# Keys, values and penalties of a dilated prompt attention stored by residue class mod 16

## What is computed

```python
DILATED_PATTERNS = ((128, 1), (512, 4), (2048, 16))
for win, dil in DILATED_PATTERNS:
    nw = win // dil                      # 128 keys per window, for each pattern
    # tokens split in dil residue classes; within a class, blocks of nw queries
    # see the block of keys before and their own, banded to dist 0..nw
    s = jnp.einsum('brnqhd,brnkhd->brnhqk', qb, kc).astype(f32) * scale + bias
    ...
    outs.append(o); lses.append(lse)
return combine_patterns(outs, lses)      # weighted by the softmax denominators
```

## Time and profile before

| What | us |
|---|---|
| median of 3 runs | 3155.96 |
| the profiled execution | 3153.91 |
| its span | 3152.2 |
| TensorE busy, mean granted clock | 2876.6, 0.947 |
| VectorE, ScalarE, GpSimd busy | 1235.5, 887.1, 192.6 |

### The profile page before, as it was taken

The page is one execution under the profiler, slowest core; times in us unless marked ns, Lnnn a source line. Parts: engine busy times, 40 slices in busy tenths (PEclk is TensorE's granted clock), DMA queues, the critical chain, the costliest instruction groups (busy, mean ns, idle before and its releaser), DMA issues. The chain is left out here.

```text
span 3152.2 us, 49398 instructions
## 1 busy us (share of the span) xinstructions
PE 2876.6 (91%) x17770; PEld 1632.3 (52%) x17770; DVE 1235.5 (39%) x2977; ACT 887.1 (28%) x2188; POOL 192.6 (6%) x476
## 2 busy tenths in 40 slices
PE   7998887673989898996997999999999999999998
PEld 6655665452657474765443444444444444444444
DVE  6326555564646465564443222222112221122134
ACT  6116666222434343443222110111001210011111
POOL 2000000100112020211110000000000000000000
PEclk9999889886989898997998999999999999999999
DMA  5121222752010201102322102111231112311035
GB/s 179 75 93 39 81 61 58 225 172 65 15 49 8 56 16 42 34 10 78 138 93 80 40 20 110 41 40 40 88 131 41 40 40 93 127 41 40 33 126 177
DMA packets 177965, 231.40 MB, mean 73 GB/s; under 512 B 12561, under 2 KB 141924, under 8 KB 177148
## 3 DMA queue, kind: packets, MB, share of 16 engines
q1 hardware_dynamic: 173142, 216.53, 21.4%
q0 software_dynamic: 4656, 12.65, 1.3%
HBM read 160.08 MB, written 69.07 MB: 73 GB/s over the span
## 5 line engine op out<-in xcount | busy, mean ns | idle before, releaser
L2312 DVE TENSOR_TENSOR f_hidden<-f_silu,f_ps_up 128x512 f32<-128x512 f32 (+1 forms) x110 | 65.2, 593 | 627.5 <-ACT f_silu L2253 627.5
L113 PE MATMUL f_ps_gate<-act_hi,f_w_hi 128*128 128x512 bf16 (+1 forms) x880 | 285.5, 343 | 11.1 <-DVE f_w_lo L2299 9.5
L113 PE MATMUL f_ps_y<-f_down_hi,f_h_hi 128*128 128x512 bf16 (+1 forms) x748 | 284.3, 380 | 8.5 <-issue 6.4
L114 PE MATMUL f_ps_gate<-act_lo,f_w_hi 128*128 128x512 bf16 (+1 forms) x880 | 285.4, 343 | 0.0
L115 PE MATMUL f_ps_gate<-act_hi,f_w_lo 128*128 128x512 bf16 (+1 forms) x880 | 285.2, 343 | 0.0
L114 PE MATMUL f_ps_up<-act_lo,f_w_hi 128*128 128x512 bf16 (+1 forms) x880 | 284.6, 342 | 0.0
L115 PE MATMUL f_ps_up<-act_hi,f_w_lo 128*128 128x512 bf16 (+1 forms) x880 | 284.6, 342 | 0.0
L113 PE MATMUL f_ps_up<-act_hi,f_w_hi 128*128 128x512 bf16 (+1 forms) x880 | 284.6, 342 | 0.0
L114 PE MATMUL f_ps_y<-f_down_lo,f_h_hi 128*128 128x512 bf16 (+1 forms) x748 | 284.3, 380 | 0.0
L115 PE MATMUL f_ps_y<-f_down_hi,f_h_lo 128*128 128x512 bf16 (+1 forms) x748 | 284.1, 380 | 0.0
L2253 ACT ACTIVATE f_silu<-f_ps_gate 128x512 f32<-128x512 f32 (+1 forms) x110 | 57.1, 519 | 656.6 <-PE f_ps_up L115 656.6
(11 more groups left out here) (360 smaller groups left out, 5483.0 us busy)
## 6 DMA issues: line engine op xcount, KB each, us to landing
y_part_rows<-f_total SPq DMA_DIRECT2D x48, 512.0 KB, 2.6
f_total<-y_part_rows SPq DMA_DIRECT2D x48, 512.0 KB, 3.5
f_raw_gate<-in_w_gate SPq DMA_DIRECT2D x22, 512.0 KB, 4.5
f_raw_up<-in_w_up SPq DMA_DIRECT2D x22, 512.0 KB, 5.9
f_raw_down<-in_w_down SPq DMA_DIRECT2D x22, 512.0 KB, 3.6
m_w_raw<-in_w_in SPq DMA_DIRECT2D x20, 512.0 KB, 5.1
s_comb<-pattern_rows SPq DMA_DIRECT2D x24, 396.0 KB, 4.4
nx<-in_x_prompt SPq DMA_DIRECT2D x16, 512.0 KB, 3.5
```

What stands on the lines that cost most here:

```text
L113: pe.matmul(out, w_hi, x_hi, start=first, stop=False)
L114: pe.matmul(out, w_hi, x_lo, start=False, stop=False)
L2312: nc.vector.tensor_tensor(hidden[u][:, 0:n], act_out[u][:, 0:n], ps_up[u][:, 0:n], ALU.mult).then_inc(hidden_done, 1)
```

## The change

Keys of the prompt are stored by residue class mod 16: class r takes 128 neighbouring places, in order of token. A key block of pattern 0 is then 16 runs of 8 keys, one of pattern 1 four runs of 32, one of pattern 2 one run of 128. Values are loaded so that their rows match that order, and the table of penalties has its columns permuted. Pattern 1 still reads its queries with stride 4; for pattern 2 GpSimd copies the queries of a pair to class order (`a_q_cls`). Penalties are loaded per sequence instead of per pair, and two waits on the new semaphore `q_sorted` are added.

```diff
+RUN = (P // CLASSES, P * DILATIONS[1] // CLASSES, P)
+def key_run(keys, pat, r, b, n):
     dil = DILATIONS[pat]
+    return keys.rearrange("p (a r b i) -> p r b a i", r=dil, b=TILES // dil, i=RUN[pat])[:, r, b:b + n, :, :]
...
-                    if dil == 1:
-                        sp.dma_start(v[k % 2][:, :, :], rows.rearrange("(b i) c -> i b c", i=P)).then_inc(v_in[k % 2], 16)
-                        return
-                    for b in range(TILES // dil):
-                        src = rows[b * P * dil:(b + 1) * P * dil, :].rearrange("(i r) c -> i r c", i=P)
-                        sp.dma_start(v[k % 2][:, b * dil:(b + 1) * dil, :], src).then_inc(v_in[k % 2], 16)
+                    if pat == 2:
+                        sp.dma_start(to[:, :, :], rows.rearrange("(i r) c -> i r c", r=CLASSES)).then_inc(loaded, 16)
+                    elif pat == 1:
+                        src = rows.rearrange("(b i a r) c -> b a i r c", b=4, i=RUN[1], a=4)
+                        for b in range(4):
+                            for a in range(4):
+                                sp.dma_start(to[a * RUN[1]:(a + 1) * RUN[1], b * 4:(b + 1) * 4, :], src[b, a]).then_inc(loaded, 16)
+                    else:
+                        src = rows.rearrange("(b i r) c -> r i b c", b=TILES, i=RUN[0])
+                        for r in range(CLASSES):
+                            sp.dma_start(to[r * RUN[0]:(r + 1) * RUN[0], :, :], src[r]).then_inc(loaded, 16)
...
                     if 2 * step + 2 == sequence_end[k]:
                         if k + 2 < len(sequence_end):
                             values(k + 2)
-                        if k == 2:
-                            penalties(2)
+                            penalties(k + 2)
...
+            @block.gpsimd
+            def _(pool):
+                for pair in range(PAIRS):
+                    pool.wait_ge(q_done, (pair + 1) * n_q)
+                    if pair:
+                        pool.wait_ge(s_ready, pair * per_pair)
+                    for a in range(2):
+                        last = nc.gpsimd.tensor_copy(q_cls[:, a, :].rearrange("p (r i) -> p r i", r=CLASSES),
+                                                     in_classes(q_st[pair % 2][:, a, 0:SEQ]))
+                    last.then_inc(q_sorted, 1)
...
+                    if pat == 2 and units[u - 1][1] != 2:
+                        pe.wait_ge(q_sorted, pair + 1)
...
-                        q = every(q_st[pair % 2][:, a, 0:SEQ], pat, r, b)
+                        q = (q_cls[:, a, r * P:(r + 1) * P] if pat == 2 else
+                             query_tile(q_st[pair % 2][:, a, 0:SEQ], pat, r, b))
...
-                    here = slice(t * P, (t + 1) * P)
-                    nc.scalar.activation(k_hi[:, :, :, here].rearrange("p q a n -> p (q a) n"),
-                                         ps_kt[:, 0:2 * D_A].rearrange("p (h n) -> p h n", h=H_A), ACT.Copy).then_inc(k_high, 1)
+                    nc.scalar.activation(key_tile(k_hi, t), turned_keys, ACT.Copy).then_inc(k_high, 1)
...
+                        act.wait_ge(q_sorted, pair - 1)
```

More of the change, by code:

```diff
@@ L320, in key_blocks, with in_classes, key_order, query_tile @@
     return [(r, b)] if pat == 2 or b == 0 else [(r, b - 1), (r, b)]
-def every(tokens, pat, r, b, n=1):
-    dil = DILATIONS[pat]
-    return tokens.rearrange("p (i r) -> p r i", r=dil)[:, r, b * P:(b + n) * P]
+CLASSES = DILATIONS[2]
+RUN = (P // CLASSES, P * DILATIONS[1] // CLASSES, P)
+def in_classes(tokens):
+    return tokens.rearrange("p (i r) -> p r i", r=CLASSES)
+def key_run(keys, pat, r, b, n):
+    dil = DILATIONS[pat]
+    return keys.rearrange("p (a r b i) -> p r b a i", r=dil, b=TILES // dil, i=RUN[pat])[:, r, b:b + n, :, :]
+def key_order(pat):
+    run = RUN[pat]
+    return [(n % run) * (P // run) + n // run for n in range(P)]
+def query_tile(tokens, pat, r, b):
+    dil = DILATIONS[pat]
+    return tokens.rearrange("p (i r) -> p r i", r=dil)[:, r, b * P:(b + 1) * P]
 def stage_prompt_attention(nc, g, sems):
@@ L338, in stage_prompt_attention @@
     rows_of = lambda t: P if t < TILES else NSAMP
-    value_loads = lambda k: sum(1 if i % 3 == 0 else TILES // DILATIONS[i % 3] for i in range(k % 2, k + 1, 2))
+    value_loads = lambda k: sum(1 if i % 3 == 2 else CLASSES for i in range(k % 2, k + 1, 2))
     PT, PROBS, STAGES = 3, 3, 3
@@ L363, in stage_prompt_attention @@
         pt_lo = [sb(f"a_pt_lo{i}", [P, CHUNK], BF16) for i in range(PT)]
-        bias = [sb(f"a_bias{i}", [P, 2, BAND_COLS]) for i in range(2)]
+        bias = [sb(f"a_bias{i}", [P, 2, 2 * P]) for i in range(2)]
         stage = [sb(f"a_stage{i}", [P, 4, 2, ROW]) for i in range(STAGES)]
@@ L492, in scores @@
                         n = len(key_blocks(pat, r, b))
-                        q = every(q_st[pair % 2][:, a, 0:SEQ], pat, r, b)
+                        q = (q_cls[:, a, r * P:(r + 1) * P] if pat == 2 else
+                             query_tile(q_st[pair % 2][:, a, 0:SEQ], pat, r, b))
                         for k, first in ((k_hi, True), (k_lo, False)):
-                            mm = nc.tensor.matmul(ps_s[u % 2][:, at:at + n * P], q, every(k[:, pair, a, :], pat, r, b + 1 - n, n),
+                            mm = nc.tensor.matmul(ps_s[u % 2][:, at:at + n * P], q, key_run(k[:, pair, a, :], pat, r, b + 1 - n, n),
                                                   start=first, stop=not first)
@@ L678, in keep_keys @@
                     dve.wait_ge(k_high, t + 1)
[L679 to L682, removed]
+                    nc.vector.tensor_tensor(key_tile(k_lo, t), turned_keys, key_tile(k_hi, t), ALU.subtract).then_inc(k_done, 1)
                 def keep_queries(pair, i):
@@ L702, in mask_scores @@
                     step = u // 2
-                    if u % per_pair == 0:
-                        dve.wait_ge(bias_in[pair % 2], (pair // 2 + 1) * 16)
+                    k = sequence_of(u)
+                    if u == 0 or sequence_of(u - 1) != k:
+                        dve.wait_ge(bias_in[k % 2], (k // 2 + 1) * 16)
                     if u % 2 == 0 and step >= STAGES:
@@ L712, in mask_scores @@
                         n = len(key_blocks(pat, r, b)) * P
-                        off = BAND_AT[pat] + BAND[pat] - n
+                        off = BAND[pat] - n
                         last = nc.vector.tensor_tensor_reduce(
-                            probs[u % PROBS][:, at:at + n], ps_s[u % 2][:, at:at + n], bias[pair % 2][:, a, off:off + n], -1.0, 3e38,
+                            probs[u % PROBS][:, at:at + n], ps_s[u % 2][:, at:at + n], bias[k % 2][:, a, off:off + n], -1.0, 3e38,
                             ALU.add, ALU.min, stage[step % STAGES][:, j, a, HD_A + 1:ROW])
@@ L2406, in weight_log @@
         return np.where(count > 0, np.log(np.maximum(count, 1)), far_away)
[L2409 to L2412, removed]
+    bands = []
+    for pat, dil in enumerate(DILATIONS):
+        order = np.array(key_order(pat))
+        keys = np.concatenate([order - P, order]) if BAND[pat] > P else order
+        dist = np.arange(P)[:, None] - keys[None, :]
+        bands.append(np.where((dist >= 0) & (dist <= P), dist * dil, -1))
     dist = np.concatenate(bands, axis=1)
```

18 lines of the change are left out of this document (11 added, 7 removed).

## The result

The changed kernel takes 3162.11 us (median of 19 runs, 3154.24 to 3168.27), the one before in the same comparison 3155.71 (19 runs, 3151.43 to 3160.87). The ratio is 1.0019, 95% interval 1.0012 to 1.0026: some 6 us slower. The forecast was 3173, 17.4 us slower; direction right, loss almost three times too large. The profiled execution took 3158.32 us with a span of 3156.4, at a mean granted clock of 0.945.

The account below looks back on a forecast made before the run. TensorE, busy 91% of the span, bounds the kernel; in prompt attention a ScalarE-TensorE loop or TensorE, with SyncE's queue on the path after the change. Losses 35.6 less gains 18.2: 17.4 us slower, from 3153.91 plus 2.05 to 3173; range 3144 to 3198.

Parts of the forecast that it names:

- Scores: TensorE's score matmuls: 0.11 us each in pattern 1, about 0.44 for eight in pattern 2, pattern 0 unchanged.
- Gain: Prompt attention, faster scores: 6.2 us in pattern 1, 1.6 and 10.4 in pattern 2, together 18.2, bounds 8 and 18.2.
- Pattern 0's loads: SyncE's queue: 16 loads to 8 partitions delay stores that masking awaits in pattern 2; 12 us twice, 24 lost.
- D - 8: Loss per stall from pattern 0's loads, queued at pattern 1's end: D less 8 us, 12 each, two times.
- D: Time the 16 loads hold up SyncE's queue: 20 us for pattern 0's loads, 10.1 for pattern 1's.
- Pattern 1's loads: SyncE's queue at pattern 2's end: 16 loads to 32 partitions delay stores; 5.1 us twice, 10.2 lost.
- D - 5: Loss per stall from pattern 1's loads: D less 5 us, 5.1 each, two times; the present 2.6 stall is counted in it.
- The start: 32 loads ahead of the first bias load put first masking at 243 to 248: 4 us lost, bound 0.
- (a): Rival, SyncE's queue: loads to few partitions run at issue rate, D = 10; net 6 us faster, 3150; chance 0.26.
- (b): Rival, SyncE's queue: issue costs a store's 0.36 and data keep up, D = 5.8; 19 us faster, 3137; chance 0.06.
- (c): Rival, SyncE's queue: rate in proportion to partitions, D = 75; two stalls of 67, about 3320; chance 0.04.
- (d): Rival, scores: pattern 1 gains 0 or pattern 0's runs cost as stride 4 did; about 3180; chance 0.11.

Follow-up runs that it names:

- e11: Changed kernel, pattern 0's sixteen value loads of 8 partitions written sixteen partitions apart instead of to 8 neighbours: 3153.93 us, ratio 0.9991.
- e3: Kernel before the change, with 16 value loads each in patterns 0 and 1, each filling all 128 partitions with one block: 3161.5 us, ratio 1.0031.
- e7: Changed kernel without GpSimd's copies, so pattern 2's queries are read with stride 16: one run, 3158.83 us.
- e12: Changed kernel, both sets of sixteen value loads cut to one block on all 128 partitions per load, values in the right places: 3166.88 us, ratio 1.0031.
- e5: Changed kernel, pattern 0's values in 8 loads of 16 partitions lying eight apart, instead of 16 loads to 8 neighbours: 3150.91 us, ratio 0.9987.
- e1: Changed kernel with values loaded as in the kernel before (1, 4 and 1 DMAs): 3140.68 us, ratio 0.9961.
- e2: Kernel before the change with only the value loads cut: 16 to 8 partitions (pattern 0), 16 to 32 (pattern 1): 3173.07 us, ratio 1.0057.

## Why the prediction was right or wrong

**Scores: right.** 0.11 us each in pattern 1, and 0.45 (0.61 less the pipeline's 0.16) for the eight of pattern 2; pattern 0's runs are free. The prediction put the cost as doubling with each halving of neighbours; by its own rows it doubles with each fourfold stride (0.43, 0.88, 1.85 ns a column), which changed none of its terms. The Trainium skill's rule on cachelines (SBUF — State Buffer, the box in the section on the DMA port swizzle) would have left pattern 1 no gain; the trace disagrees, 0.225 us having become 0.11.

**Gain: 14.6 for 18.2.** ScalarE's copies, one per unit, in pair 2's pattern 2:

```profile
534.33 0.60 ACT L652 ACTIVATE a_pt_hi<-a_ps_t 128x512 bf16<-128x512 f32 x1 [0.47 <-PE a_ps_t L551]
536.84 0.60 ACT L652 ACTIVATE a_pt_hi<-a_ps_t 128x512 bf16<-128x512 f32 x1 [0.47 <-PE a_ps_t L551]
539.81 0.60 ACT L652 ACTIVATE a_pt_hi<-a_ps_t 128x512 bf16<-128x512 f32 x1 [0.93 <-PE a_ps_t L551]
```

The period is 2.51, forecast 2.52, and then 2.97. By these starts, pattern 1 gave 1.7 and 3.3 (forecast 1.9 and 4.3), pattern 2 of pair 2 0.9 (1.6). In pairs 0 and 1 pattern 2, cleared of its waits, gave 4.2 and 3.3 for 5.2 each. Another 1.2 us came back elsewhere, half of it in the last unit. Part of the shortfall is the clock, as the prediction had warned. The window that answers to the earlier trace rows:

```profile
326.00:346.00 20.00, 12.19 (x127) 10.23 (x125) 9.32 (x53) 11.49 (x34) 7.70 (x2) 0.64 0.51 90
```

Part of it is at 0.50, the 1.2 GHz level, and units there took 2.97 where 2.51 would do. The two such periods in pair 2 after 536.84 have the same cause:

```profile
538.00:545.00 7.00, 5.66 (x50) 5.00 (x51) 3.92 (x24) 4.96 (x16) 0.00 (x0) 0.53 0.16 48
```

**Pattern 0's loads: the step that failed.** The loss was written as D - 8 with D = 20, the time for which the sixteen loads hold up the queue: 12 us twice. Both numbers were off. From first load to the store's landing there were 18.05 and 20.37 us (319.93 to 337.98, 428.90 to 449.27); less the 3.9 for what is behind the loads, D was 14.2 and 16.5. The masking waited 4.43 and 6.75 us, and the stage lost 4.2 and 5.6, together 9.8 where 24 stood. So a store landing after 13.9 and 14.8 us would have done no harm, and not only one after 11.95: the units between were longer than the sum had them (3.04, 4.88, 3.76 and 2.97 us in pair 0), some at the low clock. With the measured D and the forecast's 8 the loss would have been 14.6, so 9.4 us of the error are D and 4.8 the threshold.

What failed first is the size of D; at 14.2 and 16.5 it stood at the lower edge of the forecast's own 15 to 27. The rate to 8 partitions was put between 110 GB/s (halved once) and 14 (in proportion to 128 partitions), at 52. The windows say 66 to 69. The mechanism held in part, a slow load to few partitions, but the row that carried it was the wrong one: the step from 128 to 64 partitions in the earlier trace rows isn't the one that counts, since e11 fills 8 spread partitions at 102 to 109, bound by issue. Being neighbours is what counts, 66 for 8 and 121 for 16; no run shows 32, since pattern 1's loads are bound by their issue. The Trainium skill's estimate (SBUF — State Buffer, the DMA port swizzle: 8 neighbours on two ports, 54 GB/s, 19.7 us) had this cause right and is a fifth under the measured rate. What the prediction cites from the Trainium skill (DMA: Bandwidth & Descriptors, on why a DMA increments by 16), a leading dimension of 8 on 8 engines, is not decided here: the busy share is 0.62 for 8 neighbours and 1.23 for 16, but 0.61 for e3's 128 partitions too. It is not what slows the loads, for e11 has the same leading dimension and 102 GB/s.

**Pattern 1's loads: right in sum.** D - 5 with 10.1 was 5.1 each; D was 9.1 and 8.3, the waits 4.51 and 3.78, and with the delayed units after them the stage lost 7.95 more than before, for 10.2 - 2.6 = 7.6 forecast.

**The start: nothing for 4.** The bias landed in time: the first masking, at 240.33, waited for the scores, and from the first load to the first unit's copy there are 27.49 us, before 27.47. The 32 loads were issued in 19.75 us (215.32 to 235.07), where the forecast had 25 to 30 for the loads with their data. The margin was small: e7, with the same loads, takes 28.75 us on this path, and e12, whose 32 issues take 22.4 us, 31.35. In the traces the units do start 0.74 us later than before, but the first load already starts 0.72 later; in all the runs it starts between 214.01 and 215.40, in kernels of either layout, so that is no effect of the change. With a tenth in the first unit it makes 0.85.

**Not foreseen: 2.1.** One unit of pattern 1 in pair 0, whose copy starts at 288.75, took 3.01 us, before 2.14, and TensorE's clock is what differs. The windows after and before:

```profile
286.00:288.00 2.00, 2.00 (x9) 1.13 (x7) 1.24 (x5) 1.30 (x4) 0.00 (x0) 0.50 0.62 158
```
```profile
286.00:288.00 2.00, 2.00 (x24) 1.41 (x23) 1.11 (x6) 1.42 (x5) 0.00 (x0) 1.00 0.26 76
```

TensorE is busy throughout in both, at a granted clock of 0.50 after the change and of 1.00 before. The bias load that the change puts there is not the cause: e5 has it, keeps 1.00, and the unit takes 2.13; e3 hasn't, falls to 0.50, and it takes 3.10. Why the clock fell there stays open. TensorE had stood for 2.51 us before that unit, but so it had in e5, and in e3 only for 1.58. Over all units (from 240 us to the last copy) the mean granted clock is 0.88, before 0.91, in e1 0.92 and in e2 0.88: it goes with the waits for stores and not with the faster scores. The other 1.2 us come with a wait of 1.33 for a store at 505.70. There a new bias load (2.40 us to issue) stands before the stores, but e3, without it, waits 1.07 at the same place and the kernel before 0.59, so it explains a part at most.

**The sum.** Lost by the trace: 9.8 + 7.95 + 0.85 + 2.1 = 20.7; less 14.6 it is 6.1, and the ratio gives 6. Of the 11.3 that the forecast's 17.4 was too high, pattern 0's loads are 14.2 and the start 3.15 (4 less the 0.85); gains that were 3.6 short, 2.1 not foreseen and 0.35 for pattern 1's loads go the other way. So errors of 17.4 us one way met 6.1 the other, and the right sign is partly luck: with pattern 0's loads and the start at what they were and all other terms as forecast, the sum would have been 18.25 lost for 18.2 gained, no change. The rivals: (a), the loads at issue rate, holds for the issue (9.35 us, D = 10 in its words) but not for the data behind it; (b) and (c) are excluded by D, (d) by the score matmuls.

## What to carry to other kernels

Where a load shares a queue with stores that free buffers, price it by how long it holds up the next store, data included, and compare that with when the buffer is wanted: the loss begins at a threshold, here some 10 us, and a factor of two in rate is worth nothing under it and all above it. A load cut into few neighbouring partitions is the slow cut; stepping the same rows across the partitions takes no more code, and handing the pieces out behind successive stores, early enough for their reader, took away the rest. Before an operand is copied into order, find out which of the two the stride slows down.

## What the runs showed of the hardware

Bf16 keys as moving operand cost 0.43 ns a column in runs of 8, 32 or 128, and 0.88 and 1.85 at strides 4 and 16; the stationary operand's stride 16 costs 37 to 52 ns more per weight load (150 against 113 and 98) and 0.08 us on eight matmuls. Writing to 8 neighbouring partitions ran at 66 to 69 GB/s in the changed kernel (e2: 67 and 81), to 8 partitions sixteen apart at 102 to 109 (bound by issue), to 16 neighbours at 118 to 121, to 16 partitions eight apart at 190 to 198, in pieces of 520 B. With 16 neighbours the DMA engines' share is 1.23 at 121 GB/s, with 16 apart 0.92 at 198: by the byte, neighbours keep them busy more than twice as long. A load of a set of sixteen cost 0.47 us (e3) to 0.77 us (e12, pair 1) to issue, most where its data ran at 76 GB/s: issue time is not a constant of the queue, and seems to hold a wait for the data. GpSimd copies 2048 bf16 columns with stride 16 in 3.89 us. TensorE at a granted clock of 0.50 took 2.97 us for units of 2.51.
